# Two gated feed-forwards in fp32 on one core: the seven-product scheme in both, with adding transfers, and a row of a norm moved into the next norm's epsilon

## The chip, the cores and the metric

One core of a Trainium2 chip. The time is device microseconds of one execution, the median of the runs shown; less is better. The engines are PE (TensorE, with PEld its weight load), DVE (VectorE), ACT (ScalarE), POOL (GpSimd) and SP, which here only issues transfers.

## What is computed

Two transformer blocks one after the other on 512 tokens of width 1024 in fp32. Each ends in a gated feed-forward of inner width 2816; the rest (convolution, mLSTM, retention, attention) is not touched by the change.

```python
# first block
h = rms_norm(x, norm_ffn_g) * (1.0 + sc2) + sh2
gt, up = split(h @ w_ffn_up)
x = x + g2 * ((silu(gt) * up) @ w_ffn_down)
# second block
hn = rmsnorm(h, pre_ffn_norm)
ff = (silu(hn @ w_gate) * (hn @ w_up)) @ w_down
h = h + rmsnorm(ff, post_ffn_norm)
e = rmsnorm(p @ w_ple_proj, ple_norm)
h = h + e * sigmoid(h @ w_ple_gate + b_ple_gate)
```

`rmsnorm(x, w)` is `x * rsqrt(mean(x*x) + EPS) * w`, with EPS 1e-6.

## The kernel before

Activations lie with features on the partitions and the 512 tokens along the row. An fp32 product is made of three products of rounded halves: a weight tile of 128 x 1024 (`raw`, four buffers) is rounded by ACT into `sph`, DVE subtracts to get `spl` (L2337), and PE sums sph x high, spl x high (L1784, L1785) and sph x low (L1792) of the activations over eight k-tiles. One such **unit**, 24 matmuls of 128x512, makes one bank, that is 128 outputs of all tokens. The feed-forward's inner width is 22 tiles **f** of 128, and each f takes two units, gate and up. The results go as `midh` (MH) and `midl` (ML) into the down product.

**The seven-product scheme** runs in the first feed-forward for f = 3 to 13 (`SEVEN = {1: (3, 14)}`). It takes an f's two units as 2x2 blocks (gate and up against the two halves of k, the two halves of the tokens on the other side) and makes seven block products in place of eight: product s = 7 i + step for the i-th such f, each 12 matmuls of 128x256 (L1813, L1814, L1822). Its weight factors are half tiles: steps 0, 1 and 6 take a half as it is, steps 2 to 5 a sum of halves (`seven_sum`, DVE, L2618 to L2627, in `sums`). Each factor is then rounded (`seven_high`, ACT, L2161) and subtracted (`seven_low`, DVE, L2635). `sums` and `spl` are the same memory, a ring of six half tiles, so factor s waits for product s - 6. On the other side four sums of quarters of the activations are made once from the full activations `PF` (`seven_t_sum`, `seven_t_high`, `seven_t_low`: `ts`, `th`, `tl`). The products are joined on the way out of the banks by `seven_copy` (ACT), `seven_gate`, `seven_up` (two instructions) and `seven_last` (DVE); `seven_mid` multiplies silu(gate) by up in two halves and `seven_mid_low` (L2670) makes ML.

**What sets the order.** `plan()` writes one list of steps, and each engine runs its own in that order, waiting on semaphores. In `sevens`, at product s, `factors` adds the factor s + 5, then `drain` adds what is left of the f before, then come the joins of this f and the product itself. So DVE takes factors, joins and products of TMP in one fixed order, and anything that waits holds back all behind it. In front of the sevens, `gemms` runs f = 0 to 2 as plain units; the callback `halves(n)` of the n-th unit adds the steps that make `ts`, `th` and `tl`.

**The second feed-forward** (`ffn_up(2, ...)`) is plain throughout. It does not wait for its norm: HH and HL hold x times the gain, and the norm's row (`RROW`, one factor for each token, out of `ffn_rows`) is multiplied in afterwards, into gate before the silu (L2676) and into the product (L2689). The first three units are interleaved (`together=3`), two more follow, and then their five banks are evacuated in turn, since the row comes only then. Beside its units 4 to 12 lie `e_squares`: the eight squares (ACT) and sums (DVE, L2343) of the embedding `EE`, and a ninth call that turns the sum on PE (L1872) and takes the root.

Of the rings TMP has six rows, the main banks are five in the second feed-forward, RAW has four buffers. BY_DMA units (6 to 23, before the part that is told of here) get their `spl` by a transfer from POOL that adds into its destination (L2974).

## Time and profile before

| | us |
|---|---|
| median of 3 runs (1569.41 to 1570.70) | 1569.88 |
| the profiled execution | 1569.71 |
| its span, first to last instruction | 1567.9 |
| PE busy | 1539.4 |
| DVE busy | 1053.9 |
| ACT busy | 698.2 |
| POOL busy | 107.3 |
| sevens of the first feed-forward, 554.0 to 673.1 | 119.0 |
| same f in the second, 1186.7 to 1306.3 | 119.7 |

The profiled execution is 0.17 us under the median, and 1.8 us of it lie outside the span. A row of the timeline gives start, duration, engine, line, operation and tiles, and in brackets how long the engine had been idle and what ended that. Neighbouring instructions of one engine overlap in the records: a DVE row of 0.68 us is followed by the next after 0.60. The mean granted clock of PE was 0.997.

### The profile page before, as it was taken

Reading aid. Unit: us, or ns where it says so; the run is one execution under the profiler, and the core shown is the slowest. Engines: PE = TensorE matmul, PEld = TensorE weight load, DVE = VectorE, ACT = ScalarE, POOL = GpSimd, SP = SyncE. Lnnn points to the kernel's source line nnn. Section 1 sums busy time; section 2 is a strip of 40 time slices with the busy share of each in tenths; the row PEclk is TensorE's granted clock in tenths of the full one; section 3 lists DMA queues with packets and bytes.
Section 4 is the critical chain, followed back from the end, with each engine's and each line's share of the span. In section 5 each row is a group of like instructions: output and inputs, shape, how many; then the busy total and the mean of one; then the engine's idle time right before and its main releaser. Section 6 shows DMA issues by size and latency. Waiting matters only on the chain.

```text
span 1567.9 us, 19025 instructions
## 1 busy us (share of the span) xinstructions
PE 1539.4 (98%) x7320; PEld 1266.2 (81%) x7320; DVE 1053.9 (67%) x1631; ACT 698.2 (45%) x1025; POOL 107.3 (7%) x100
## 2 busy tenths in 40 slices
PE   8999899999999999999999999999999999999998
PEld 3788778877888899988888887778888888888877
DVE  7998898887887799954563547766486544442346
ACT  5543578764542655532233335446354332222233
POOL 0111000000000100000011001000201011000000
PEclk9999999999999999999999999999999999999999
DMA  9787222223565323344333323211333322233331
GB/s 371 177 206 183 75 88 63 83 83 118 191 242 171 131 82 96 94 142 143 102 111 101 108 84 109 66 42 41 114 112 106 105 95 94 97 95 101 98 134 67
DMA packets 54092, 185.10 MB, mean 118 GB/s; under 512 B 6381, under 2 KB 8685, under 8 KB 53746
## 3 DMA queue, kind: packets, MB, share of 16 engines
q1 hardware_dynamic: 51056, 173.39, 33.8%
q0 software_dynamic: 2944, 10.50, 3.5%
q8 instruction: 58, 0.95, 0.3%
q14 instruction: 32, 0.26, 0.0%
q10 hardware_dynamic: 2, 0.00, 0.0%
HBM read 169.70 MB, written 4.20 MB: 111 GB/s over the span
## 4 chain that ended last, share of the span: by engine, by line
PE 82%; DVE 12%; ACT 3%; issue 2%; DMA 0%; ACTq 0%; DVEq 0%; POOL 0%; POOLq 0%
PE bank L1792 23%; PE bank L1784 23%; PE bank L1785 23%; DVE convout L2391 2%; PE bank L1840 2%; DVE tmp L2462 1%; PE bank L1852 1%; PE bank L1854 1%; PE bank L1853 1%; PE bank L1927 1%; PE bank L1944 1%; DVE spl L2337 1%; DVE spl L2635 1%; PE bank L1957 1%; PE bank L1950 1%
## 5 line engine op out<-in xcount | busy, mean ns | idle before, releaser
L1784 PE MATMUL bank<-HH,sph 128*128 128x512 f32 x1256 | 499.9, 398 | 6.9 <-DVE spl L2337 4.7
L1785 PE MATMUL bank<-HH,spl 128*128 128x512 f32 x1256 | 490.7, 391 | 0.0
L2337 DVE TENSOR_TENSOR spl<-raw,sph 128x1024 fp32r<-128x1024 f32 (+1 forms) x214 | 269.4, 1260 | 238.2 <-ACT sph L2002 238.1
L1792 PE MATMUL bank<-HL,sph 128*128 128x512 f32 x1256 | 325.5, 394 | 0.0
L2002 ACT ACTIVATE sph<-raw 128x1024 fp32r<-128x1024 f32 (+1 forms) x235 | 241.5, 1029 | 177.8 <-PE bank L1792 141.2
L1784 PEld LDWEIGHTS bank<-HH,sph 128*128 128x128 f32 x1256 | 236.6, 188 | 60.7 <-issue 9.5
L1785 PEld LDWEIGHTS bank<-HH,spl 128*128 128x128 f32 x1256 | 236.7, 188 | 50.1 <-issue 1.2
L1792 PEld LDWEIGHTS bank<-HL,sph 128*128 128x128 f32 x1256 | 234.7, 188 | 51.1 <-issue 2.4
L2391 DVE SCALAR_TENSOR_TENSOR convout<-convin,vecs,convout 128x512 f32<-128x512 f32 x240 | 164.9, 742 | 0.0
L1784 PE MATMUL bank<-midh,sph 128*128 128x512 f32 x352 | 136.9, 389 | 0.0
L1785 PE MATMUL bank<-midh,spl 128*128 128x512 f32 x352 | 136.9, 389 | 0.0
L1792 PE MATMUL bank<-midl,sph 128*128 128x512 f32 x352 | 87.6, 389 | 0.0
L2204 ACT ACTIVATE midh<-tmp 128x512 fp32r<-128x512 f32 x33 | 20.9, 633 | 127.7 <-DVE tmp L2689 87.9
L1785 PEld LDWEIGHTS bank<-midh,spl 128*128 128x128 f32 x352 | 66.1, 188 | 13.7
L1792 PEld LDWEIGHTS bank<-midl,sph 128*128 128x128 f32 x352 | 66.1, 188 | 13.7
L1784 PEld LDWEIGHTS bank<-midh,sph 128*128 128x128 f32 x352 | 66.1, 188 | 13.7
L2979 POOL TENSOR_TENSOR tmp<-tmp,tmp 128x512 f32<-128x512 f32 x27 | 35.2, 1313 | 509.0 <-ACT tmp L2017 509.0
L1813 PE MATMUL bank<-th,sph 128*128 128x256 f32 x176 | 45.1, 289 | 5.6 <-DVE tmp L2652 4.3
L2462 DVE SCALAR_TENSOR_TENSOR tmp<-xpad,vecs,tmp 128x512 f32<-128x512 f32 x48 | 36.0, 749 | 16.6 <-ACT tmp L2061 15.5
L2161 ACT ACTIVATE sph<-sums 128x512 fp32r<-128x512 f32 x44 | 27.8, 632 | 38.4 <-DVE sums L2627 16.7
L3012 POOL TENSOR_TENSOR midl<-tmp,midh 128x512 fp32r<-128x512 f32 x22 | 28.5, 1296 | 230.3 <-ACT midh L2204 230.3
L1814 PE MATMUL bank<-th,spl 128*128 128x256 f32 x176 | 44.0, 283 | 0.0
(359 smaller groups left out, 2118.8 us busy)
## 6 DMA issues: line engine op xcount, KB each, us to landing
raw<-in_w_in SPq DMA_DIRECT2D x69, 512.0 KB, 3.6
raw<-in_w_up SPq DMA_DIRECT2D x66, 512.0 KB, 3.5
more<-in_w_ada SPq DMA_DIRECT2D x32, 512.0 KB, 4.7
raw<-in_w_down SPq DMA_DIRECT2D x32, 512.0 KB, 3.5
raw<-in_w_gate SPq DMA_DIRECT2D x22, 512.0 KB, 3.2
spl<-raw POOLq DMA_DIRECT2D x18, 512.0 KB, 6.0
ada<-in_w_ada SPq DMA_DIRECT2D x16, 512.0 KB, 11.3
raw<-in_w_down SPq DMA_DIRECT2D x16, 384.0 KB, 3.1
```

Source lines behind the costliest of these rows:

```text
L1784: e.matmul(P_[b][:], sph(n)[:, q], hi[:, k, :], start=k == 0, stop=False)
L1785: e.matmul(P_[b][:], spl(n)[:, q], hi[:, k, :], start=False, stop=False)
L1792: m = e.matmul(P_[b][:], sph(n)[:, q], low[:, k, :], start=False, stop=last and k == kb - 1)
L1813: e.matmul(to, high_of(which, s)[:, q], x, start=k == 0, stop=False)
L1814: e.matmul(to, low_of(which, s)[:, q], x, start=False, stop=False)
L1840: m = e.matmul(P_[b][:], raw(n)[:, token(k)], FULL[acts][:, k, :], start=k == 0, stop=k == 7)
L2002: e.activation(sph(n), raw(n), ACT.Copy).then_inc(*up("s_w_high", ("wh", n)))
L2337: e.tensor_tensor(spl(n), raw(n), sph(n).bitcast(F32), ALU.subtract).then_inc(*up("s_w_low", ("wl", n)))
L2391: ins = e.scalar_tensor_tensor(CO[:, i, :], src, wt, CO[:, i, :], ALU.mult, ALU.add)
L2462: e.scalar_tensor_tensor(TMP[j][:], XP[:, s, k:k + 512], wt, TMP[j][:], ALU.mult, ALU.add).then_inc(*up("s_qk_conv", ("qk_conv", h, z, k)))
L2979: e.tensor_tensor(TMP[a][:], TMP[a][:], TMP[j][:], ALU.add).then_inc(*up("s_sum_p", ("ss", name, i)))
L3012: e.tensor_tensor(ML[:, i, :], TMP[j][:], MH[:, i, :].bitcast(F32), ALU.subtract).then_inc(*up("s_cut_p", ("lo", "m2", i)))
```

## The change

1. `SEVEN` gets the second feed-forward too, for the same f = 3 to 13. `PF` is there x times the gain (ACT, 8 instructions), DVE makes `ts` and `tl`, ACT `th`, as in the first. In `seven_gate` and `seven_last` the norm's row is multiplied in on half the width each (`seven_scaled`).
2. Of the four weight sums three remain. The sum of the two first halves is made by a transfer that POOL issues, which adds one half onto the other in `raw` (`seven_third`, 256 KB for each f). The signs of some factors are turned, and `seven_mid` multiplies by -1 in the same instruction. The second factor's low part now waits for the third sum, because both use the memory of the first sum.
3. `seven_mid_low` leaves DVE: ACT writes -MH into ML and a transfer from POOL adds TMP to it (256 KB for each f).
4. In the second feed-forward the row is no longer multiplied into the up side. So the down product is off by a factor for each token, which its own norm takes out again once its epsilon is EPS times (mean(x*x) + EPS) of the norm before: `ff_eps` keeps that in `KEEP`, and the root of `ff` adds it in place of EPS.
5. `e_squares` moves from units 4 to 12 into the sevens: steps 1, 3 and 5 of the first three f. `EE` moves by 4096 bytes.

```diff
-SEVEN = {1: (3, 14)}
-SEVEN_SUMS = (2, 3, 4, 5)
-SEVEN_BANK = ((0, 0), (1, 0), (2, 1), (1, 1), (3, 1), (2, 0), (3, 0))
+SEVEN = {1: (3, 14), 2: (3, 14)}
+SEVEN_SUMS = (2, 3, 4)
+SEVEN_BANK = ((0, 0), (1, 0), (1, 1), (2, 1), (3, 1), (2, 0), (3, 0))
...
             add("seven_high", st["which"], s)
-            if s:
+            if s % 7 == 4:
+                factor_low(st, s - 2)
+            if s and s % 7 != 3:
                 factor_low(st, s - 1)
...
+            if step == 5 and i + 2 < f1 - f0:
+                add("seven_third", which, i + 2)
+            if which == 2 and i < 3 and step in (1, 3, 5):
+                e_squares()
...
         def halves(n):
-            if n == 1:
+            if n in (3, 5):
+                add("seven_third", which, (n - 3) // 2)
+            if which == 2 and n < 2:
+                for i in range(4 * n, 4 * n + 4):
+                    add("seven_full", which, i)
+            elif n == 1:
                 for i in range(0, 8, 2):
                     add("seven_full", which, i)
+            if n == 1:
                 add("seven_t_sum", which, 0)
...
             def seven_low(which, s):
                 w.wait_ge(at("seven_high", which, s))
+                if s % 7 == 2:
+                    w.wait_ge(at("seven_sum", which, s + 2))
...
+                if which == 2:
+                    w.wait_ge(at("seven_gate", 2, i), at("rrow", 2))
+                    e.tensor_tensor(TMP[j][:, 0:256], TMP[j][:, 0:256], RROW[:, 0:256], ALU.mult).then_inc(
+                        *up("s_ffn", ("seven_scaled", i, 0)))
...
-                    e.tensor_tensor(TMP[j][:], TMP[j][:], P_[b][:], ALU.mult).then_inc(*up("s_ffn", ("up", 2, i)))
-                    w.wait_ge(at("up", 2, i))
-                    e.tensor_tensor(TMP[j][:], TMP[j][:], RROW[:], ALU.mult).then_inc(
-                        *up("s_ffn", ("up_done", 2, i)))
+                    e.tensor_tensor(TMP[j][:], TMP[j][:], P_[b][:], ALU.mult).then_inc(
+                        *up("s_ffn", ("up", 2, i), ("up_done", 2, i)))
...
+            def seven_third(which, i):
+                n = seven_at[which][0] + 2 * i
+                w.wait_ge(at("raw", n), at("raw", n + 1))
+                e.dma_start(raw_half(n + 1, 0), raw_half(n, 0), accum_op=ALU.add).then_inc(
+                    *G.up(f"d_third{i % 2}", ("seven_third", which, i), by=16))
+
+            def seven_mid_low(which, i, f, j):
+                w.wait_ge(at("less", f"m{which}", f))
+                e.dma_start(ML[:, f, :], TMP[j][:], accum_op=ALU.add).then_inc(
+                    *G.up(f"d_mid{f % 4}", ("lo", f"m{which}", f), by=16))
```

Where instructions now stand, in three places. `raw` and `spl` carry the number of their buffer.

DVE at the start of the second feed-forward, before: from the product of f = 0 on, its evacuations and the first of the sums of `EE`.

```order
L2687 TENSOR_TENSOR tmp_91<-tmp_91,bank 128x512 [waits s_gate,s_product]
L2689 TENSOR_TENSOR tmp_91<-tmp_91,rrow 128x512 [waits s_ffn]
L2676 TENSOR_TENSOR tmp_90<-bank,rrow 128x512 [waits s_product]
L2687 TENSOR_TENSOR tmp_90<-tmp_90,bank 128x512 [waits s_gate,s_product]
L2689 TENSOR_TENSOR tmp_90<-tmp_90,rrow 128x512 [waits s_ffn]
L2676 TENSOR_TENSOR tmp_88<-bank,rrow 128x512 [waits s_product]
L2337 TENSOR_TENSOR spl_63<-raw_56,sph_60 128x1024 [waits s_w_high]
```

The same engine and place in the changed kernel, from the product of f = 0 to the low part of factor 1 (the last row).

```order
L2726 TENSOR_TENSOR tmp_91<-tmp_91,bank 128x512 [waits s_gate,s_product]
L2633 TENSOR_TENSOR ts<-pf 128x1024 [waits s_cut_a,s_w_low]
L2715 TENSOR_TENSOR tmp_90<-bank,rrow 128x512 [waits s_product]
L2636 SCALAR_TENSOR_TENSOR ts<-pf,ts 128x1024 [waits s_cut]
L2726 TENSOR_TENSOR tmp_90<-tmp_90,bank 128x512 [waits s_gate,s_product]
L2646 TENSOR_TENSOR tl<-ts,th 128x1024 [waits s_cut_a]
L2641 SCALAR_TENSOR_TENSOR ts<-pf,ts 128x1024 [waits s_cut]
L2715 TENSOR_TENSOR tmp_88<-bank,rrow 128x512 [waits s_product]
L2646 TENSOR_TENSOR tl<-ts,th 128x1024 [waits s_cut_a]
L2638 TENSOR_TENSOR ts<-pf 128x1024
L2655 TENSOR_TENSOR sums_66<-raw_56 128x512 [waits d_third0,d_raw2]
L2671 TENSOR_TENSOR spl_62<-raw_55,sph_59 128x512 [waits s_w_high]
```

Six instructions of 1024 columns and two waits on other engines (`s_cut_a` is ACT, `d_third0` the transfer) now stand between the evacuation of f = 0 and the low part of factor 1. Behind the last row follow the sum for factor 3, one product, two more `tl`, the third sum, and only then the low part of factor 2.

ACT at the same place, before: the silu of each gate and the high part of each product.

```order
L2199 ACTIVATE tmp_91<-tmp_91 128x512 [waits s_ffn]
L2204 ACTIVATE midh<-tmp_91 128x512 [waits s_w_low,s_w_high,s_ffn]
L2199 ACTIVATE tmp_90<-tmp_90 128x512 [waits s_ffn]
L2204 ACTIVATE midh<-tmp_90 128x512 [waits s_ffn]
L2199 ACTIVATE tmp_88<-tmp_88 128x512 [waits s_ffn]
```

And in the changed kernel.

```order
L2223 ACTIVATE tmp_91<-tmp_91 128x512 [waits s_ffn]
L2156 ACTIVATE pf<-XT,vecs 128x512 [waits s_w_low,s_w_high]
L2156 ACTIVATE pf<-XT,vecs 128x512 x3
L2228 ACTIVATE midh<-tmp_91 128x512 [waits s_ffn]
L2156 ACTIVATE pf<-XT,vecs 128x512 x4
L2223 ACTIVATE tmp_90<-tmp_90 128x512 [waits s_ffn]
L2165 ACTIVATE th<-ts 128x1024 [waits s_cut]
```

The eight `pf` stand behind the first silu and in front of the second, and the first `ts` on DVE waits for all of them.

DVE in the second feed-forward beside the sums of `EE` (L2343), before: each sum stands between the split of a whole unit and an evacuation.

```order
L2337 TENSOR_TENSOR spl_61<-raw_57,sph_58 128x1024 [waits s_w_high]
L2676 TENSOR_TENSOR tmp_86<-bank,rrow 128x512 [waits s_product]
L2343 TENSOR_TENSOR tmp_87<-tmp_87,tmp_89 128x512 [waits s_sum,s_square]
L2337 TENSOR_TENSOR spl_62<-raw_54,sph_59 128x1024 [waits s_w_high]
L2687 TENSOR_TENSOR tmp_86<-tmp_86,bank 128x512 [waits s_gate,s_product]
L2689 TENSOR_TENSOR tmp_86<-tmp_86,rrow 128x512 [waits s_ffn]
```

In the changed kernel they (now L2367) stand between the factors of the sevens; here most of the second f of the sevens.

```order
L2367 TENSOR_TENSOR tmp_87<-tmp_87,tmp_90 128x512 [waits s_sum,s_square]
L2655 TENSOR_TENSOR sums_64<-raw_56 128x512 [waits d_third0,d_raw2,s_product]
L2671 TENSOR_TENSOR spl_63<-raw_55,sph_60 128x512 [waits s_w_high]
L2676 TENSOR_TENSOR tmp_88<-tmp_86,bank 128x512 [waits s_gate]
L2682 TENSOR_TENSOR tmp_88<-tmp_88,rrow 128x256 [waits s_ffn]
L2658 TENSOR_TENSOR sums_64<-sums_64,raw_55 128x512 [waits s_w_low,d_raw1,s_product]
L2367 TENSOR_TENSOR tmp_87<-tmp_87,tmp_89 128x512 [waits s_sum,s_square]
L2661 TENSOR_TENSOR sums_65<-raw_55,sums_64 128x512 [waits s_product]
L2671 TENSOR_TENSOR spl_61<-sums_64,sph_58 128x512 [waits s_w_low,s_w_high]
L2671 TENSOR_TENSOR spl_61<-sums_64,sph_58 128x512 [waits s_w_high]
L2687 TENSOR_TENSOR tmp_86<-tmp_88,bank 128x512
```

Each waits for a square on ACT, and all factors of the f behind it wait with it. On PE the turn of the finished sum, which waits for the last of them, stands in front of product 19, step 5 of the third f.

## Rows read from the trace of the kernel before

**Rows 1.** The page, first part: busy time and share of the span.

```profile
PE 1539.4 (98%) x7320; PEld 1266.2 (81%) x7320; DVE 1053.9 (67%) x1631; ACT 698.2 (45%) x1025; POOL 107.3 (7%) x100
```

**Rows 2.** Windows: from:to, length, then busy time of each engine, clock, transfers.

```profile
554.00:673.00 119.00, 113.35 (x925) 111.31 (x924) 111.77 (x192) 62.89 (x117) 0.00 (x0) 1.00 0.32 98
1187.00:1306.00 119.00, 119.00 (x529) 98.52 (x528) 60.64 (x67) 42.77 (x57) 15.12 (x12) 1.00 0.29 98
```

**Rows 3.** The chain of waits in order: start, length; ends of two neighbouring units.

```profile
1184.84 1.81 PE bank L1792 x8
1190.28 1.81 PE bank L1792 x8
```

**Rows 4.** Timeline of PE in the sevens: products 0, 1 and 3, first unit behind.

```profile
554.02 0.28 PE L1813 MATMUL bank<-HH,sph 128*128 128x256 f32 x1
...
555.45 0.28 PE L1813 MATMUL bank<-HH,sph 128*128 128x256 f32 x1
...
559.82 0.39 PE L1813 MATMUL bank<-th,sph 128*128 128x256 f32 x1 [1.34 <-DVE spl L2635]
...
673.05 0.40 PE L1784 MATMUL bank<-HH,sph 128*128 128x512 f32 x1
```

**Rows 5.** Waits of PE in the sevens: us in total, times, longest.

```profile
PE bank L1813 <- DVE tmp L2652: 4.3, 9, 0.5
```

**Rows 6.** Timeline of DVE, one round of the sevens.

```profile
614.42 0.69 DVE L2635 TENSOR_TENSOR spl<-raw,sph 128x512 fp32r<-128x512 f32 x1 [0.41 <-ACT sph L2161]
615.03 0.42 DVE L2662 TENSOR_TENSOR tmp<-tmp,tmp 128x256 f32<-128x256 f32 x1
615.37 0.42 DVE L2665 TENSOR_TENSOR tmp<-tmp,tmp 128x256 f32<-128x256 f32 x1
```

**Rows 7.** Timeline of DVE at the start of the sevens: sum and low part.

```profile
558.48 0.69 DVE L2624 TENSOR_TENSOR sums<-raw,sums 128x512 f32<-128x512 f32 x1
559.09 0.68 DVE L2635 TENSOR_TENSOR spl<-sums,sph 128x512 fp32r<-128x512 f32 x1
```

**Rows 8.** Timeline of the first gate of the second feed-forward, DVE and ACT.

```profile
1180.17 0.69 DVE L2676 TENSOR_TENSOR tmp<-bank,rrow 128x512 f32<-128x512 f32 x1
1180.90 0.63 ACT L2199 ACTIVATE tmp<-tmp 128x512 f32<-128x512 f32 x1 [2.19 <-DVE tmp L2676]
```

**Rows 9.** Timeline of the first feed-forward, the instructions that make PF, TS and TH.

```profile
536.28 2.55 ACT L2143 ACTIVATE pf<-pf,mod 128x512 f32<-128x512 f32 x4
...
539.11 1.22 DVE L2596 TENSOR_TENSOR ts<-pf 128x1024 f32<-128x1024 f32 x1 [2.01 <-ACT pf L2143]
540.25 1.22 DVE L2337 TENSOR_TENSOR spl<-raw,sph 128x1024 fp32r<-128x1024 f32 x1
...
540.37 1.06 ACT L2148 ACTIVATE th<-ts 128x1024 fp32r<-128x1024 f32 x1
```

**Rows 10.** The page: POOL's ML; transfers (KB, median us to landing).

```profile
L3012 POOL TENSOR_TENSOR midl<-tmp,midh 128x512 fp32r<-128x512 f32 x22 | 28.5, 1296 | 230.3 <-ACT midh L2204 230.3
...
raw<-in_w_up SPq DMA_DIRECT2D x66, 512.0 KB, 3.5
...
spl<-raw POOLq DMA_DIRECT2D x18, 512.0 KB, 6.0
...
tmp<-m_scratch POOLq DMA_DIRECT2D x4, 256.0 KB, 4.1
```

**Rows 11.** Sums of EE in 1187 to 1306 by form; and the reciprocal behind them.

```profile
L2343 DVE TENSOR_TENSOR tmp<-tmp,tmp 128x512 f32<-128x512 f32 x7 | 7.5, 1078 | 8.5 <-ACT tmp L2017 8.5
...
1227.69 0.18 DVE L2359 RECIPROCAL small<-small 128x4 f32<-128x4 f32 x1 [1.42 <-ACT small L2022]
```

**Rows 12.** The longest wait of PE within the kernel, and the windows behind it.

```profile
179.03 0.76 PE L1784 MATMUL bank<-HH,sph 128*128 128x512 f32 x1 [4.74 <-DVE spl L2337]
...
180.00:182.00 2.00, 2.00 (x6) 1.59 (x5) 1.83 (x7) 0.00 (x0) 0.00 (x0) 0.50 0.70 248
184.00:186.00 2.00, 2.00 (x10) 1.66 (x9) 1.90 (x5) 1.97 (x4) 0.47 (x1) 1.00 0.00 0
```

More of the change, by code:

```diff
@@ L165, in split @@
     def split():
-        n = W["cut"]
+        c = n = W["cut"]
         for st in stages:
-            if st["first"] <= n < st["first"] + st["slots"]:
-                factors(st, 2 * (n - st["first"]) + 2)
+            if st["first"] <= c < st["first"] + st["slots"]:
+                factors(st, 2 * (c - st["first"]) + 2)
                 W["cut"] += 1
                 return
-            if n >= st["first"] + st["slots"]:
+            if c >= st["first"] + st["slots"]:
                 n -= st["slots"] - st["units"]
@@ L426, in rsqrt @@
         add("rsqrt", name, src, v, q, r, n, scale, after)
+        if name == "x4":
+            add("ff_eps", v)
         return r
@@ L945, in ffn_up @@
             jobs += part(i)
-        if which == 2:
-            jobs = [(*job[:3], e_squares) if 4 <= n < 13 else job for n, job in enumerate(jobs)]
         if not st:
@@ L977, in ffn_up @@
             gemm(src, tile_no, 8, acts, evac)
-            if n % 2:
+            if n % 2 and which == 1:
                 ada_more(1 if ada_at[0] < 32 else 0)
@@ L1520, in program @@
         PTL = place("ptl", B + 8192, [128, 2, S], F32R)
-        EE = place("ee", B + 16384, [128, 8, S])
+        EE = place("ee", B + 12288, [128, 8, S])
         PTS_0 = place("pts0", B + 65536, [128, 2, S])
@@ L2141, in seven_full @@
             def seven_full(which, i):
+                if which == 2:
+                    w.wait_ge(at("x", 4, i), *fenced("f2"))
+                    e.activation(PF[:, i, :], XT[:, i, :], ACT.Copy, scale=vec("g_pf", i)).then_inc(
+                        *up("s_cut_a", ("full2", i)))
+                    return
                 w.wait_ge(at("lo", "n2", i))
@@ L2158, in seven_high @@
                 else:
-                    w.wait_ge(at("raw", n if s % 7 < 2 else n + 1))
+                    w.wait_ge(at("seven_third", which, s // 7) if s % 7 == 5 else at("raw", n if s % 7 < 2 else n + 1))
                     given = undivided(which, s)
@@ L2180, in seven_mid @@
                 w.wait_ge(at("seven_mid", which, i), *fenced(f"f{which}"))
+                if which == 2:
+                    w.wait_ge(at("e_spilt"))
                 e.activation(MH[:, f, :], TMP[j][:], ACT.Copy).then_inc(*up("s_cut_a", ("hi", f"m{which}", f)))
+            def seven_mid_low(which, i, f, j):
+                w.wait_ge(at("hi", f"m{which}", f))
+                e.activation(ML[:, f, :], MH[:, f, :].bitcast(F32), ACT.Copy, scale=-1.0).then_inc(
+                    *up("s_cut_a", ("less", f"m{which}", f)))
             def gmix(i):
@@ L2616, in seven_sum @@
                 if s % 7 == 2:
-                    w.wait_ge(at("raw", n + 1))
+                    w.wait_ge(at("raw", n + 1), at("seven_third", which, s // 7))
                     ins = e.tensor_tensor(to, raw_half(n + 1, 0), raw_half(n + 1, 1), ALU.add)
```

73 lines of the change are left out of this document (42 added, 31 removed).

## The prediction

> **What bounds the kernel now.** I read the busy shares first. PE is busy 98% of the span [rows 1], so a gain must come out of PE's work or of one of its few gaps. Next I compared two windows of equal length with the same eleven tiles f = 3 to 13: the first feed-forward with the seven-product scheme, the second without it [rows 2]. The reader is to see two different limits. In the second PE has no gap (119.0 of 119.0), and DVE is half idle (60.6). In the first PE lacks 5.7 us, and DVE is busy 111.8 of 119.0: the scheme takes matmuls from PE and gives DVE almost all that it can do. The timeline of PE [rows 4] and its waits [rows 5] say who holds it: ten gaps, all ended by DVE.
>
> **Prices of PE.** A plain unit takes 5.44 us (1184.84 to 1190.28, [rows 3]), an f two of them, 10.88. A product of the scheme takes 1.44 us (554.02 to 555.45, [rows 4]), an f seven, 10.08. Eleven f: 119.7 against 110.9. So the scheme is worth 8.8 us in a feed-forward, if nobody waits.
>
> **First feed-forward.** It took 119.0 us (554.02 to 673.05, [rows 4]), so 8.1 over 110.9. Of these 1.5 came before product 3, which began at 559.82 and not at 558.34; the other 6.6 are DVE's. From product 3 on, 74 products took 113.2 us, 10.7 for each f: that is DVE's round. An instruction of 512 columns takes 0.60 us of it from start to start (558.48 to 559.09, [rows 7]), one of 256 columns 0.34 [rows 6]. The change takes out one weight sum and the ML instruction, 1.2 us, so the round falls to some 9.5, under PE's 10.08, and the 6.6 us go. In exchange the low part of factor 2 must wait for the third sum. That sum stood at 558.48 [rows 7], behind the last `tl`, and I find nothing that moves it; the low part then ends at about 559.8, and product 2 begins there and not at 556.9. Product 3 follows at 561.25, 1.4 later than before. Gain 5.2 us. Bounds: 3 (a round nearer 10.08, or a cold clock after the wait of 2.9 us, below) to 6.6.
> The two new transfers for each f lie beside this. ACT has room for its extra instruction (62.9 of 119, [rows 2]). For the landing of 256 KB the trace has two neighbours, 4.1 us for a plain transfer of that size and 6.0 for an adding one of twice the size [rows 10]; I take 4.5 and keep 4.1 to 6.0. The last factor of an f frees the second raw buffer, its load lands 3.5 us later [rows 10], and by the plan the sum that needs the added half comes some 8 us behind that: hidden.
> The Trainium skill (DMA: Bandwidth & Descriptors, "Anatomy of one DMA — SWDGE (gpsimd) path") fits such a transfer as 2.0 us plus its bytes over 436 GB/s, an estimate of 2.6 us here. The row of 6.0 us for 512 KB is nearly twice what that fit gives (3.2), so the trace disagrees; by the page the sum would be 0.8 us lower, in the next part.
>
> **Second feed-forward, start.** It gains 8.8 us by PE's prices. But the order shows what stands in front of its first products. The first gate is scaled by the norm's row at 1180.2, and its silu ends at 1181.5 [rows 8]. Only then does ACT take the eight `pf` (0.64 each, from 2.55 for four, [rows 9]) and one high part: 5.6 us, to 1187.1. The first `ts` waits for all eight. From there DVE has eleven instructions to the low part of factor 1: six of 1024 columns at 1.14 (539.11 to 540.25, [rows 9]) and five at 0.60, 9.8 us, to 1197.0. The added half comes somewhat later still: POOL issues it behind its second ML (1.3 us, [rows 10]), which waits for the high part of f = 1 at about 1191.4, so at 1192.8, and lands it at 1197.3; with 0.8 us for that, factor 1 is ready at 1197.8. PE finishes the last plain unit at 1186.65 [rows 3], product 0 at 1188.1, and waits 9.7 us.
> Then come one sum, one product of TMP and one `tl` (2.4 us), a wait of 0.6 for the last `th`, which ACT makes (1.06, [rows 9]) behind two factors and a high part, the last `tl`, the third sum and the low part of factor 2 (2.3): 1203.1. Product 2 was due at 1189.5. **Loss 13.6 us**; bounds 12.4 (`pf` at 0.53, the added half in time) to 15.5 (it lands after 6.0).
>
> **The sums of EE.** From product 2 of the first f to product 2 of the fourth DVE decides, so I add up its rounds, low part of factor 2 to low part of factor 2. Without EE a round has 13 instructions at 0.60, five halves at 0.34 (two are the new scaling), some 0.4 for steps that depend on the one before, and the wait of 0.4 for ACT [rows 6]: 10.3. Each sum of EE adds 0.60 and a wait for its square, which stands on ACT behind factors. Before, that wait was 1.2 on average (8.5 over 7, [rows 11]) and cost nothing. The first round has no joins of an f before it and stays inside PE's 10.08, with 0.7 to spare. Following the rows of the second, with three sums, I find waits of 0.9, 1.6 and 1.2 for their squares, in place of the 0.4: 15.4. In the third a root with its trip to ACT (1.4, [rows 11]) stands for one sum: 16.0. Together 31.4 against 20.2, less 0.7: **loss 10.5 us**, 5 of it at one place, where PE is to turn the finished sum in front of product 19 and waits for the last sum. Bounds 6 (no wait for squares) to 15 (their waits half as long again). Behind the third f the round of 10.3 costs up to 0.2 for each of eight f, less what the cold clock gives DVE: 0.5, bounds 0 to 3.
>
> **The clock.** After PE's wait of 4.74 us the granted clock was 0.50, 1.2 of 2.4 GHz, and 1.00 again at 184 [rows 12]; a window of 2 us held 6 matmuls in place of 10, so some 4.4 us at half pace, about 2.2 us lost. In the changed kernel two waits are as long or longer, 9.7 us and 5. I take 3.5 for both, since part of the first is hidden by the wait before product 2; bounds 0 to 6.6 with the first feed-forward's.
>
> **Epsilon.** In the plain f one DVE instruction goes and one tiny one is added; DVE is half idle there [rows 2], so nothing. What it spares in the sevens is counted above.
>
> **Sum**, against the profiled execution's 1569.7, which is the median within 0.2: -5.2 - 8.8 + 13.6 + 10.5 + 0.5 + 3.5 = +14.1, **1583.8 us**.
>
> **Rivals.** A: the scheme pays in both, because DVE and ACT find time that I don't see: -5.2 - 8.8 gives 1555.7. For it speaks that DVE is half idle in the second window; against it that the start is a fixed order with the row at 1180.2, and no idle time of the average can be moved in front of that.
> B: only the start costs, and the sums of EE slip into waits that PE has anyway: -14.0 + 13.6 + 1 gives 1570.3. Against it: after product 2 PE and DVE run at the same pace, so an instruction more on DVE is a wait on PE.
> C (slower than the forecast): the added halves come late in every f. By the 8 us above, it decides at a landing of about 8 us; at 9.5 us, 1.5 us in each of 20 f, 30 us, 1613. Against it: beside a DVE that was almost never idle, 512 KB landed in 6.0 [rows 10].
> The Trainium skill (GPSIMD Engine Reference, the table of its specifications) says that GpSimd shares its SBUF interfaces with VectorE and contends with instructions that have two SBUF inputs, which most here are. By that rule C gains; the trace shows no such delay in the rows of 6.0.
>
> **How the numbers follow.** Forecast 0.72, A 0.08, B 0.14, C 0.06. The forecast's own bounds: the gains 14.0 against 12.4 + 6 gives 1574.1, 11.8 against 15.5 + 15 + 3 + 3.5 gives 1595, with all bad ends together. The range must reach B and may leave out A, C and the last of the bad ends: 1570 to 1592. A measurement of this kernel can tell about 0.2%, 3.1 us, from no change. Faster than 1566.7: A and a little of B, 0.10. Within: most of B, 0.13. Slower than 1573.0: 0.77.
>
> **What would show it.** Right: in the first sevens no more gaps ended by the second half of `seven_up` (L2652 before), one gap of 2.9 us before product 2 and an end near 113.8 us after the start; in the second a gap of 9 to 10 us before product 1 ended by DVE, one of 3 to 4 before product 2, one of about 5 at the turn of EE's sum, a clock of 0.50 behind the first, and 135 to 142 us for the eleven f. Wrong: product 1 soon after 1188, gaps ended by a DMA in every f, or a DVE round in the first sevens that stays at 10.7.

## The result, and the profile after

| | before | changed |
|---|---|---|
| median of 4 runs each | 1569.64 us | 1593.41 us |
| lowest to highest | 1568.89 to 1570.70 | 1592.59 to 1593.88 |
| ratio | | 1.0148, 95% interval 1.0135 to 1.0160 |

The changed kernel is slower by 23.8 us. The forecast was +14.1 (1583.8), its range ended at 1592.0: direction and places were right, the sum was 9.6 us short.

The page of the changed kernel, first part (compare [rows 1]): PE has hardly more work, DVE and ACT have 47 us more each.

```profile
PE 1540.1 (97%) x7716; PEld 1285.2 (81%) x7716; DVE 1101.4 (69%) x1750; ACT 744.9 (47%) x1136; POOL 131.2 (8%) x133
```

Its windows over the two sevens (columns as in [rows 2]; the last three numbers are granted clock, share of the transfers, GB/s): the first are filled by PE, in the second PE lacks 23 us, DVE is busy in 125 of 145, and the mean clock is 0.92.

```profile
555.00:671.00 116.00, 113.03 (x928) 112.75 (x927) 101.81 (x172) 67.71 (x129) 16.33 (x19) 0.99 0.57 144
1184.00:1329.00 145.00, 121.58 (x931) 118.42 (x929) 124.57 (x212) 79.73 (x148) 20.70 (x23) 0.92 0.46 117
```

PE's waits from 1184 to 1332 (us in total, times, longest). Every one was ended by DVE, none by a transfer, and L2652's nine in the first sevens [rows 5] are gone.

```profile
PE bank L1825 <- DVE spl L2671: 15.9, 3, 10.2
PE bank L1884 <- DVE tmp L2367: 5.0, 1, 5.0
PE bank L1825 <- DVE tmp L2676: 2.0, 1, 2.0
PE bank L1796 <- DVE spl L2361: 1.5, 1, 1.5
```

The timeline of PE puts them in place. The rows are product 0 and 2 of the first sevens and the unit behind these (compare [rows 4]); then of the second sevens product 0, 1, 2, 9, 15, 16, the turn of EE's sum ahead of product 19, product 23, and the first plain unit behind.

```profile
555.39 0.28 PE L1825 MATMUL bank<-HH,sph 128*128 128x256 f32 x1
...
561.39 0.39 PE L1825 MATMUL bank<-th,sph 128*128 128x256 f32 x1 [2.97 <-DVE spl L2671]
...
670.98 0.40 PE L1796 MATMUL bank<-HH,sph 128*128 128x512 f32 x1
...
1184.43 0.28 PE L1825 MATMUL bank<-HH,sph 128*128 128x256 f32 x1
...
1196.22 0.55 PE L1825 MATMUL bank<-HH,sph 128*128 128x256 f32 x1 [10.20 <-DVE spl L2671]
...
1202.08 0.58 PE L1825 MATMUL bank<-th,sph 128*128 128x256 f32 x1 [2.96 <-DVE spl L2671]
...
1214.72 0.28 PE L1825 MATMUL bank<-th,sph 128*128 128x256 f32 x1
...
1225.55 0.38 PE L1825 MATMUL bank<-HH,sph 128*128 128x256 f32 x1 [2.03 <-DVE tmp L2676]
...
1229.97 0.39 PE L1825 MATMUL bank<-th,sph 128*128 128x256 f32 x1 [2.74 <-DVE spl L2671]
...
1239.73 0.69 PE L1884 MATMUL bank<-consts,tmp 128*128 128x128 f32 x2 [4.97 <-DVE tmp L2367]
...
1248.43 0.28 PE L1825 MATMUL bank<-th,sph 128*128 128x256 f32 x1
...
1330.42 0.50 PE L1796 MATMUL bank<-HH,sph 128*128 128x512 f32 x1 [1.54 <-DVE spl L2361]
```

**Where the 23.9 us between the two profiles lie.** I cut every profile at the same four marks of PE: product 0 of the first sevens; the first matmul of the first down product; the turn of the second norm's sums (the four small matmuls ahead of the second feed-forward); the first matmul of the second down product. A is the stretch between the first two, B between the last two.

| us | product 0 at | A | between | B | behind |
|---|---|---|---|---|---|
| before | 554.02 | 206.10 | 414.53 | 219.05 | 174.20 |
| changed | 555.39 | 202.66 | 414.52 | 245.02 | 174.21 |

So -3.4 in A, +26.0 in B, and +1.4 ahead of product 0. That last piece isn't the change's: in kernels that are the same up to there product 0 stood between 553.2 and 555.4.

**B by rows of PE.** 77 products at 1.44 would be 110.9, 8.8 under before. From product 0 to product 2 it took 17.65, 14.8 more than two products; from 2 to 23 46.35, 16.1 more than 21; from 23 to the end of 76 (1328.71) 80.28, 2.5 more; and 1.5 of gap behind. -8.8 + 14.8 + 16.1 + 2.5 + 1.5 = +26.1.

### The profile page after: what moved, and what is told of

Read it like the earlier page. It is cut to its first block, busy times and chain, and to the rows that moved or that the text cites. A ratio compares the mean times of both kernels' runs of the same rounds, so it can differ in the third digit from the quotient of the medians.

```text
span 1591.8 us, 20216 instructions
## 1 busy us (share of the span) xinstructions
PE 1540.1 (97%) x7716; PEld 1285.2 (81%) x7716; DVE 1101.4 (69%) x1750; ACT 744.9 (47%) x1136; POOL 131.2 (8%) x133
## 4 chain that ended last, share of the span: by engine, by line
PE 79%; DVE 13%; ACT 4%; issue 2%; DMA 1%; ACTq 0%; DVEq 0%; POOL 0%; POOLq 0%
PE bank L1796 20%; PE bank L1804 20%; PE bank L1797 20%; PE bank L1825 2%; PE bank L1834 2%; PE bank L1826 2%; DVE convout L2425 2%; PE bank L1852 2%; DVE spl L2671 2%; DVE tmp L2496 1%; PE bank L1864 1%; PE bank L1866 1%; PE bank L1865 1%; PE bank L1939 1%; DVE spl L2361 1%
## 5 line engine op out<-in xcount | busy, mean ns | idle before, releaser
L1796 PE MATMUL bank<-HH,sph 128*128 128x512 f32 x1080 | 431.3, 399 | 8.8 <-DVE spl L2361 6.4
L1797 PE MATMUL bank<-HH,spl 128*128 128x512 f32 x1080 | 422.0, 391 | 0.0
L1804 PE MATMUL bank<-HL,sph 128*128 128x512 f32 x1080 | 282.0, 395 | 0.0
L1825 PE MATMUL bank<-th,sph 128*128 128x256 f32 x352 | 93.0, 295 | 9.1 <-DVE spl L2671 8.7
L1826 PE MATMUL bank<-th,spl 128*128 128x256 f32 x352 | 91.5, 290 | 0.0
L1825 PEld LDWEIGHTS bank<-th,sph 128*128 128x128 f32 x352 | 70.1, 199 | 11.6 <-DVE spl L2671 10.6
L1825 PE MATMUL bank<-HH,sph 128*128 128x256 f32 x264 | 67.3, 287 | 12.2 <-DVE spl L2671 10.2
L1826 PEld LDWEIGHTS bank<-th,spl 128*128 128x128 f32 x352 | 70.2, 200 | 0.0
L1826 PE MATMUL bank<-HH,spl 128*128 128x256 f32 x264 | 66.9, 285 | 0.0
L2671 DVE TENSOR_TENSOR spl<-raw,sph 128x512 fp32r<-128x512 f32 x88 | 60.2, 688 | 7.8 <-ACT sph L2178 7.5
```

Of the source, the lines that this page charges most:

```text
L1796: e.matmul(P_[b][:], sph(n)[:, q], hi[:, k, :], start=k == 0, stop=False)
L1797: e.matmul(P_[b][:], spl(n)[:, q], hi[:, k, :], start=False, stop=False)
L1804: m = e.matmul(P_[b][:], sph(n)[:, q], low[:, k, :], start=False, stop=last and k == kb - 1)
L1825: e.matmul(to, high_of(which, s)[:, q], x, start=k == 0, stop=False)
L1826: e.matmul(to, low_of(which, s)[:, q], x, start=False, stop=False)
L2671: e.tensor_tensor(low_of(which, s), given, high_of(which, s).bitcast(F32), ALU.subtract).then_inc(*up("s_w_low", ("seven_low", which, s), ...
```

## The experiments

All are compared with the kernel before, on the same chip. For sevens that begin one f later A begins 10.88 later too; in the table that is added.

| kernel | median us | ratio to before, 95% | A | B |
|---|---|---|---|---|
| e1_first_only | 1566.45 | 0.9975 (0.9966 to 0.9985) | 201.17 | 219.08 |
| e2_no_sums | 1578.31 | 1.0051 (1.0036 to 1.0066) | 201.16 | 231.48 |
| e3_warm | 1592.27 | 1.0141 (1.0126 to 1.0156) | 201.17 | 247.02 |
| e4_early | 1590.35 | 1.0127 (1.0112 to 1.0142) | 202.65 | 243.04 |
| e5_warm_turn | 1589.97 | 1.0131 (1.0116 to 1.0146) | 201.16 | 243.48 |
| e6_no_scale | 1584.27 | 1.0098 (1.0083 to 1.0113) | 202.67 | 237.57 |
| e7_late_second | 1574.51 | 1.0026 (1.0013 to 1.0039) | 203.70 | 226.22 |
| e8_late_first | 1563.39 | 0.9959 (0.9945 to 0.9974) | 199.69 | 219.07 |
| e9_sums_later | 1586.69 | 1.0104 (1.0089 to 1.0119) | 202.65 | 238.95 |
| e10_both_late | 1570.29 | 1.0002 (0.9993 to 1.0011) | 199.68 | 225.75 |
| e11_row_on_pool | 1574.71 | 1.0033 (1.0020 to 1.0046) | 199.69 | 229.58 |
| e12_from_five | 1577.72 | 1.0048 (1.0031 to 1.0064) | 199.68 | 234.03 |
| e13_silu_later | 1588.90 | 1.0115 (1.0098 to 1.0132) | 202.44 | 240.02 |
| e14_from_five | 1564.67 | 0.9965 (0.9952 to 0.9978) | 199.70 | 220.23 |
| e15_from_eight | 1562.83 | 0.9951 (0.9936 to 0.9966) | 199.70 | 216.98 |
| e16_turn_later | 1559.66 | 0.9932 (0.9920 to 0.9944) | 199.69 | 214.56 |
| e17_five_turn_later | 1565.93 | 0.9972 (0.9961 to 0.9983) | 199.69 | 221.63 |

### Which half of the change costs: e1

```diff
-SEVEN = {1: (3, 14), 2: (3, 14)}
+SEVEN = {1: (3, 14)}
...
+        if which == 2:
+            jobs = [(*job[:3], e_squares) if 4 <= n < 13 else job for n, job in enumerate(jobs)]
```

> The second feed-forward plain again, with the sums of EE back in its units 4 to 12; all the rest of the change stays (adding transfers in the first feed-forward, the row moved into the epsilon). Theory: everything lost was lost in the second sevens. The first sevens take 115.6 us as in the changed kernel (119.0 before), the second feed-forward is as before, and the 1.4 us by which the first sevens start later in the profile of the change stay if they come from the change: 1567.5, or 1566.2 if they don't. Rival: the transfers or the epsilon cost something outside the sevens: 1570 or more.

Measured 1566.45, B as before: the whole loss is the second sevens', and transfers and epsilon cost nothing outside them. A is 4.9 under before, not 3.4. PE waits the same 2.97 before product 2 as in the changed kernel, but here the clock did not fall:

```profile
563.00:565.00 2.00, 2.00 (x19) 2.00 (x18) 1.78 (x4) 0.43 (x1) 0.00 (x0) 1.00 0.36 74
```

The changed kernel in the same window: 0.50, 11 matmuls for 19.

```profile
563.00:565.00 2.00, 2.00 (x11) 2.00 (x11) 1.35 (x3) 0.72 (x2) 0.00 (x0) 0.50 0.34 94
```

So the difference of 1.5 us is the clock alone. The time lies at the 1566.2 of the expectation: the later start of product 0 is not the change's.

### The sums of EE: e2 and e9

e2 drops the calls of `e_squares`. e9 keeps them; in `e_sum` the sum of square i - 1 (`sum_held`) now goes with square i:

```diff
-        for i in range(8):
-            sse.add(("EE", i), [("e", i)])
...
+        for i in range(1, 8):
+            sum_held()
+            j, free = tmp.take()
+            add("square", "e", i, j, free, ("EE", i), [("e", i)], None)
+            held.append((i, j))
             yield
+        sum_held()
```

> The changed kernel with the squares and sums of EE left out (and its root; the last norm is spread from a kept column that does not belong to it, so the output of that norm isn't the reference's). Theory: the rounds of the second and third f lose 5.2 and 8.4 us to these sums, 2.2 of it by the cold clock behind the third wait; without them 1593.4 - 13.6 = 1579.8. Rival: DVE is too slow in the second sevens even without them, since the rounds of the later f are 10.65 us where PE needs 10.08; then the first rounds stay long and the time is above 1585.

> The changed kernel; at each of its nine places in the second sevens the square of EE is followed by the sum of the square before it, not by its own. Nothing is left out. Theory: in the trace of the change DVE stands idle 0.9 to 1.7 us in front of seven of these sums, for a square that ACT makes just ahead of it (8.9 us together), and that is more than half of what EE costs there; only the sums' own 0.6 us and the root stay: rounds of about 12 and 14.5 us for 16.0 and 16.7, time 1586, bounds 1584 to 1588. Rival: DVE's own instructions are what the rounds lack; the waits only move in front of other rows (TMP, high parts): 1590 or more.

Both came out close to their theories (1578.31 for 1579.8, 1586.69 for 1586). e2 took 13.5 us from B: EE is the largest part of what the rows between product 2 and 23 lose (46.35 became 32.43, and 21 products without a wait are 30.2). The late rounds stayed as slow as they were, so its rival is right about those alone. e9 took 6.1 from B. In the timeline of DVE in the changed kernel one sees what it removed: an idle time in front of each sum, for a square that ACT has only just begun (7 such, 8.9 us; before, 8.5 over 7 that cost nothing, [rows 11]).

```profile
1206.23 0.69 DVE L2367 TENSOR_TENSOR tmp<-tmp,tmp 128x512 f32<-128x512 f32 x1 [1.19 <-ACT tmp L2029]
...
1223.00 0.69 DVE L2367 TENSOR_TENSOR tmp<-tmp,tmp 128x512 f32<-128x512 f32 x1 [1.66 <-ACT tmp L2029]
...
1238.98 0.69 DVE L2367 TENSOR_TENSOR tmp<-tmp,tmp 128x512 f32<-128x512 f32 x1 [1.65 <-ACT tmp L2029]
```

In e9 PE runs from product 2 to 18 without a gap, where the changed kernel has two (in front of 15 and 16). The only wait of PE that EE still causes is the turn in front of product 19, now 5.7 us, with a cold clock behind it (waits of PE, 1180 to 1330):

```profile
PE bank L1840 <- DVE spl L2686: 13.7, 3, 10.2
PE bank L1899 <- DVE tmp L2382: 5.7, 1, 5.7
PE bank L1811 <- DVE spl L2376: 1.6, 1, 1.6
```

### The clock: e3 and e5

`warm_seven` is a row of matmuls into a bank that is free there; in e5 the 20 for product 19 stand ahead of `e_squares()`:

```diff
+            if (which, s) in WARM:
+                add("warm_seven", wb, wfree, WARM[which, s])
```

> The changed kernel with matmuls that nobody reads, of 512 columns at 0.23 us, put on PE ahead of the products that wait: 11 before product 2 of the first sevens, and in the second 42 before product 1, 18 before product 2, 8, 11 and 20 before products 15, 16 and 19. Theory: the cold clock behind the waits costs 1.6 + 4.0 + 2.2 = 7.8 us; a clock that stays at 1.00 gives these back, less what DVE then holds up since it loses the time in which it got ahead: 1586 to 1589. Rival (the forecast's own size): the clock costs 3.5, the rest is DVE's anyway: 1590 or more.

> As e3_warm, but the 20 matmuls stand ahead of the turn of EE's sum, where PE waits 5.0 us, and not behind it. In e3_warm they stood behind it and took 4.5 us themselves, and the wait stayed cold. Theory: the cold clock costs 1.5 in the first sevens, 1.6 net at the start of the second (of 4.0 in the rows of PE the rounds with EE give 2.4 back, since DVE holds them anyway) and 2.2 behind the turn: 1593.4 - 5.3 = 1588.1, 4 us under e3_warm. Rival: behind the turn too the time belongs to DVE; then only the wasted matmuls of e3_warm show in neither place and the time stays at 1590.3.

Both kept the clock at 1.00 behind the waits for products 1, 2, 15 and 16, as e5's window behind the first wait shows (the changed kernel's: 0.50 with 8 matmuls). At the turn only e5 did: in e3 PE waited 4.96 us there, the clock fell to 0.50 (1234 to 1238), and the 20 matmuls behind the turn ran cold themselves.

```profile
1196.00:1198.00 2.00, 2.00 (x10) 1.67 (x9) 1.93 (x2) 0.00 (x0) 1.06 (x2) 1.00 0.22 40
```

Behind each of its rows of unread matmuls e5's PE still waited 0.1 to 0.7 us for DVE, so they held nothing up. Yet B fell by only 1.5 in e5, and in e3 it rose by 2.0. The rows of PE show why. Products 3 and 4 take 1.44 again in e5, but the rounds behind are as long as before or longer: from product 2 to 23 42.96 against 46.35, and from 23 on 82.1 against 80.3, since PE now reaches sooner the pace that DVE can hold. Both theories missed (1592.27 for at most 1589, 1589.97 for 1588.1), and both rivals came true: I had taken the cold products from PE's rows and added them to waits which they partly replace. The cold clock costs 3.0 us in the whole kernel (1.5 in A, 1.5 in B), not 5.3 and not 7.8.

### DVE's round: e6, e13 and e11

e6 leaves the two multiplications by the row out. e13 leaves nothing out and moves one silu on ACT:

```diff
             if step == 0:
                 add("seven_last", which, i, banks[3][0], up[i])
+                if which == 1:
+                    add("seven_silu_last", which, i, up[i])
+            elif step == 1:
+                if which == 2:
+                    add("seven_silu_last", which, i, up[i])
```

> The changed kernel without the two multiplications by the norm's row in each f of the second sevens (their silu takes the unscaled gate, so the output isn't the reference's). Theory: a round of DVE there is 10.65 us against PE's 10.08, and the two scalings are 0.7 of it; without them the round is below PE's, and the 2.5 us that the last 33 products lose go: 1590.9. Rival: the round is held by the wait for ACT's high part (0.40) and a chain that does not shorten: 1592.5 or more.

> The changed kernel with ACT's silu of the second half of the gate one product later in the second sevens, so that it stands behind the high part that DVE waits for. Nothing is left out. Theory: DVE's round of 10.65 us holds 0.40 of waiting for that high part, because ACT waits for the scaled gate first; without it the round is 10.25, the 2.5 us that the last 33 products lose fall under 1, and the gap of 1.5 in front of the first plain unit, which comes from the same lateness, shrinks: 1593.4 - 3 = 1590.4, bounds 1589 to 1591.5. Rival: the product of TMP two steps on then waits for the later silu, and the round stays: 1593.

e6 took 7.5 from B and e13 5.0, more than either theory gave. In both PE has no gap from product 21 on, and from product 23 to 76 runs at 1.44 each; the gap behind the sevens is gone in e6 and 1.1 in e13. Another 3.1 us of e6 and 2.0 of e13 came from the rounds with EE (rows of PE from product 2 to 23), which are DVE's too. What e13 removed is this wait in DVE's round of the changed kernel (the row with the bracket; [rows 6] has the same wait, 0.41, in the kernel before). The other two rows are the scalings.

```profile
1302.74 0.42 DVE L2701 TENSOR_TENSOR tmp<-tmp,rrow 128x256 f32<-128x256 f32 x1
...
1304.17 0.69 DVE L2671 TENSOR_TENSOR spl<-raw,sph 128x512 fp32r<-128x512 f32 x1 [0.40 <-ACT sph L2178]
...
1308.07 0.42 DVE L2682 TENSOR_TENSOR tmp<-tmp,rrow 128x256 f32<-128x256 f32 x1
```

e13 has the same two low parts back to back:

```profile
1298.83 1.28 DVE L2676 TENSOR_TENSOR spl<-raw,sph 128x512 fp32r<-128x512 f32 x2
```

In the changed kernel ACT stands 2.9 us in front of that silu, waiting for the scaled gate, and the high part comes behind it. So DVE waits for ACT, which waits for DVE.

e11 takes the same two instructions off DVE by giving them to POOL:

> e10_both_late with the two multiplications by the norm's row in each f of the second sevens on POOL instead of DVE. Theory (after e6_no_scale, which gave 9.1 us without them): DVE's round falls below PE's 10.08, so neither the late rounds nor the gap behind the sevens cost anything: 3 us under e10_both_late, 1557. Rival: POOL's instruction is slower and holds its two transfers and the silu behind it, or slows DVE beside it: no gain on e10_both_late, or a loss of 1 us in each f.

The theory (1557) missed by 17.7 us. It was 4.4 us slower than e10 and B 3.8 longer, the rival's case. Two lines of the groups by form, 1220 to 1305, show one part of it: the sum that runs beside POOL's instruction. Of e10:

```profile
L2691 DVE TENSOR_TENSOR sums<-raw,sums 128x512 f32<-128x512 f32 x8 | 5.5, 684 | 0.0
```

and of e11, where it took 1162 ns:

```profile
L3042 POOL TENSOR_TENSOR tmp<-tmp,rrow 128x256 f32<-128x256 f32 x7 | 7.7, 1100 | 4.4 <-DVE tmp L2706 4.4
...
L2691 DVE TENSOR_TENSOR sums<-raw,sums 128x512 f32<-128x512 f32 x8 | 9.3, 1162 | 0.0
```

The other part is the chain: POOL's 1.1 us stands for DVE's 0.42 ahead of the silu, and DVE then waits 1.6 for the high part behind it. The Trainium skill (GPSIMD Engine Reference, the table of its specifications) says that GpSimd's SBUF interfaces are shared with VectorE and that instructions with two SBUF inputs contend; the trace agrees, 1162 ns for 684. It also shows that not every such pair is slow (timeline of e11, rows of DVE and POOL):

```profile
1250.44 0.68 DVE L2688 TENSOR_TENSOR sums<-sums,raw 128x512 f32<-128x512 f32 x1
1250.62 1.10 POOL L3042 TENSOR_TENSOR tmp<-tmp,rrow 128x256 f32<-128x256 f32 x1
1251.04 1.23 DVE L2691 TENSOR_TENSOR sums<-raw,sums 128x512 f32<-128x512 f32 x1
...
1255.84 0.69 DVE L2701 TENSOR_TENSOR spl<-raw,sph 128x512 fp32r<-128x512 f32 x1
1256.01 1.11 POOL L3048 TENSOR_TENSOR tmp<-tmp,rrow 128x256 f32<-128x256 f32 x1 [3.47 <-DVE tmp L2723]
```

The two DVE instructions that had begun ahead of POOL's took their usual time; the one that began 0.68 us before the end of POOL's took 0.54 longer.

### The starts: e4, e8, e7, e10, e12

e4, in `ffn_rows`:

```diff
         r = root_of(ss, D)
+        for i in range(8):
+            add("seven_full", 2, i)
+        add("seven_t_sum", 2, 0)
+        add("seven_t_sum", 2, 1)
```

e8, on top of e1 (10 f don't fill the ring of three weight slots evenly, so one slot is passed over):

```diff
-SEVEN = {1: (3, 14)}
+SEVEN = {1: (4, 14)}
```

> The changed kernel with the eight copies PF of the second feed-forward issued behind the squares of its norm, ahead of the first gate, the first two sums TS behind them, and TH, TL, the other TS and the first two adding transfers one unit earlier. Theory: the start of the second sevens costs 13.2 us of waits and 4.0 of clock because PF stands behind the first silu; 11 us earlier, one short wait is left and most of it goes: 1593.4 - 13 = 1580, bounds 1577 to 1584. Rival: the adding transfer, behind POOL's ML, is what ends last once DVE is early: a wait of 5 us or more stays before product 1, and the time is 1586 or more.

> e1_first_only with the sevens of the first feed-forward over f = 4 to 13 instead of 3 to 13; TS, TH and TL stay at their units, so they stand two units further ahead. Theory: the wait of 3.0 us before product 2 and the 1.6 of cold clock behind it are the work of the start not done in time; both go, one f less costs 0.8: 1566.4 - 3.8 = 1562.6. Rival: product 2 waits for the order of the new scheme itself (its low part behind the third sum), however early the start: 1566.4 + 0.8 = 1567.2.

e8 came close to its theory (1563.39 for 1562.6, -3.1 against e1 for -3.8). Its one wait of 0.7 before product 2 stands for 2.97. e4 missed (1590.35 for 1580): B fell by 2.0 and not by 13. The first TS stood on DVE waiting 5.0 for PF, ahead of the copy of the norm's row and with it of the first gate; the banks came free late, and PE stood in a plain unit instead (timeline of PE in e4):

```profile
1184.07 0.80 PE L1807 MATMUL bank<-HH,sph 128*128 128x512 f32 x1 [5.05 <-DVE tmp L2726]
```

and 5.3 more before product 1, since DVE had 12 us of work from there to the low part of factor 1. The time is in the rival's range, but not for its reason: DVE did not wait for the added half. So the start's price was not that PF came late: it was a mass of DVE work between the row and product 1. That called for more plain units ahead:

> The whole change, but the second sevens run over f = 6 to 13 only; EE's squares and sums stand in plain units 3 to 11, PF at units 1 and 2, TS, TH and TL at units 3 to 7. Theory: with twelve plain units ahead DVE has done the start's work beside them; no long wait of PE is left in the second feed-forward, and eight f give 6.4 us, of which up to 2.5 go to the DVE round of 10.65 and 1.5 to the gap in front of the first plain unit behind. Against the first feed-forward alone (1566.4): 1564, bounds 1561 to 1566. Rival: the start's waits come from the scheme itself (the adding transfer, the last TL) and not from the units ahead: 1569 or more.

> The whole change with the first sevens over f = 4 to 13 and the second over f = 6 to 13, EE's squares at plain units 2 to 10 and each sum one unit behind its square. Theory: in e7_late_second DVE stood idle 1.2 us in front of every sum of EE and 1.9 in front of TS, and its split stood behind that: PE waited 2.8 and 0.9 in plain units and 2.2 before product 2, since EE's root stood there too. All these go; what stays is the DVE round of 10.65 in the last f and the gap of 1.5 behind the sevens. Against e8_late_first: 1563.4 - 6.4 + 3 = 1560, bounds 1558 to 1563. Rival: TS, TL and the splits overfill DVE in the plain units whatever the order: 1565 or more.

> e11_row_on_pool with the second sevens from f = 5 on and EE's squares, TS, TH and TL one unit earlier. Theory: one f more in the scheme is worth 0.8 us as long as DVE finds the time ahead of it: 1556.2. Rival: the ten plain units are too few, a wait with its cold clock comes back in them or before product 2: 1559 or more.

All three missed, by 10.5, 10.3 and 21.5 us. The gap moved once more, to the plain units; e7's timeline of PE:

```profile
1192.09 0.47 PE L1811 MATMUL bank<-HH,sph 128*128 128x512 f32 x1 [2.84 <-DVE spl L2376]
```

There DVE waited for PF in front of TS, with the split of the next unit behind; in e10 the split itself waited for a high part that stood on ACT behind PF and TH (PE 3.4 late), and in e12, where DVE stood 6.8 us for PF, PE's wait in the plain unit was 6.4. On top came 2.2 before product 2 and 2.5 behind the sevens in e7, 1.4 at EE's turn and 2.5 behind the sevens in e10, and 1.6, 2.3 and e11's 0.85 in most f in e12.

### Can the second sevens pay: e14 to e17

These put four of the eight PF ahead of the norm's root, where ACT stands idle for 4 us, spread the rest over two units, and keep e9's order of the sums and e13's silu. e16 and e17 also turn EE's sum a unit later, in `e_sum`:

```diff
         sum_held()
+        yield
         b = sse.columns()
```

> The whole change with the first sevens over f = 4 to 13, the second over f = 5 to 13, and the silu as in e13. Of PF four are made ahead of the norm's root, where ACT stands idle for 4 us, the rest at units 0 and 1; EE's squares at units 1 to 9, each sum a unit later, TS, TH and TL at units 2 to 6. Theory: in e10 DVE waited 2.4 us for PF and then for a high part behind it, and PE 3.4 for that; and the sevens' padded length made the first unit behind wait for the last product (2.5). With both gone nine f give 7.2 us less 1 to 2 of drift: against e8's 1563.4, 1557.5, bounds 1556 to 1561. Rival: ten plain units hold too little of DVE's time for the start, EE and the splits: a wait of 3 us or more in them, 1563 or more.

> As e14_from_five, with the second sevens over f = 8 to 13: sixteen plain units ahead of them, EE's squares at units 4 to 12, TS, TH and TL at units 3 to 7, and no padding. Theory: nothing waits, six f give 4.8 us and DVE's longer round doesn't come through in so few: 1558.6, bounds 1557.5 to 1560.5. Rival: the plain units with TS, TL and a sum of EE are overfull (2 splits' worth more on DVE than 5.44 us hold), whatever stands behind them: 1562 or more.

> e15_from_eight with EE's squares two units earlier, the turn of its finished sum one unit behind the last sum and not right behind it, and TS, TH and TL one unit later. Theory: the gain of the six f, 4.8 us, came to only 2.1 in e15 since PE waited 1.4 for the last sum of EE in front of its turn and 0.4 for a split behind the first TS, with a cold clock behind; both go: 217.0 us from the turn of the norm's sums to the down product become 214.5, the time 1560.5. Rival: a plain unit with TS, TL and EE in it holds more DVE work than PE needs for it, and the same time is lost at another unit: 1562.5 or more.

> The same for the second sevens from f = 5 on (nine f): EE's squares from unit 0, the turn at unit 9, TS, TH and TL at units 3 to 7. Theory: e14 lost 2.9 at the turn, 1.9 in a plain unit and 1.5 to 2 by cold clocks; with these gone nine f give 7.2 us: 1558, bounds 1557 to 1561. Rival: in ten plain units EE, TS, TL and the splits together are too much for DVE: 1563 or more.

e16 met its theory (1559.66 for 1560.5); e14, e15 and e17 missed by 7.2, 4.2 and 7.9 us, and their rivals came true. e16 is the best kernel of all: 10.4 us under before, 33.8 under the change as made, and in its second feed-forward, from 1170 to 1380, PE waits for nobody. Its B, 214.56, is 4.5 under before, where six f by PE's prices are worth 4.8; another 6.4 are A's, which e8 has too without any sevens in the second feed-forward (1563.39). e14 and e17 show the other side: three f more are worth 2.4, but with ten plain units ahead, in place of sixteen, the waits come back (1.9 and 2.9 in e14; 1.6 and 3.3 in e17).

## Why the prediction was wrong, point by point

**First feed-forward (-5.2).** Right. Without the clock's fall A is 4.9 shorter, the wait before product 2 was 2.97 for the 2.9 forecast, and DVE no longer sets the pace. With the fall it is 3.4.

**Second feed-forward, PE's prices (-8.8).** Right: 1.44 for each product wherever nobody waits.

**Landing of the added half (4.5).** Under-sized, without effect. The two new transfers' medians in the changed kernel:

```profile
raw<-raw POOLq DMA_DIRECT2D x22, 256.0 KB, 5.3
midl<-tmp POOLq DMA_DIRECT2D x22, 256.0 KB, 3.2
```

5.3 lies inside the bounds of 4.1 to 6.0, and no wait of PE was ended by it; the longest took 7.6, so rival C's limit of 8 us was not reached. The estimate by the Trainium skill (DMA: Bandwidth & Descriptors, "Anatomy of one DMA — SWDGE (gpsimd) path"), 2.6 us, is half of it.

**Start (+13.6).** Right in place and nearly in size: waits of 10.20 and 2.96 where 9.7 and 3.4 were worked out, together 13.2. With the cold product between them product 2 came 14.8 late. That is DVE's time and not the clock's: e5 held the clock and took the same 17.7 us to product 2. Two errors met here, so part of the agreement is luck. DVE did not wait for the added half, for which the forecast had 0.8. And beside POOL's ML DVE's third TS took 2.29 where the second took 1.22, 1.1 that the forecast did not have.

```profile
1186.85 1.22 DVE L2636 SCALAR_TENSOR_TENSOR ts<-pf,ts 128x1024 f32<-128x1024 f32 x1
...
1189.40 1.52 POOL L3059 TENSOR_TENSOR midl<-tmp,midh 128x512 fp32r<-128x512 f32 x1 [5.61 <-ACT midh L2228]
1189.72 2.29 DVE L2641 SCALAR_TENSOR_TENSOR ts<-pf,ts 128x1024 f32<-128x1024 f32 x1
```

**The sums of EE (+10.5) and the drift (+0.5): the step that failed.** The mechanism was right, waits for the squares of 0.93, 1.66 and 1.28 in the second round (forecast 0.9, 1.6 and 1.2) and the turn of 5 (4.97), but the base under it was mis-sized. The forecast took DVE's round as 10.3. It is 10.65 (each f from product 51 on in the changed kernel, and every late f in e5), and PE's is 10.08 (the same f in e6 and e13). A late round of DVE, low part to low part (1304.17 to 1314.82), shows which terms were too small:

```profile
1306.05 0.68 DVE L2655 TENSOR_TENSOR sums<-raw 128x512 f32<-128x512 f32 x1
1306.75 0.69 DVE L2671 TENSOR_TENSOR spl<-raw,sph 128x512 fp32r<-128x512 f32 x1
...
1309.02 0.68 DVE L2661 TENSOR_TENSOR sums<-raw,sums 128x512 f32<-128x512 f32 x1
1309.81 1.29 DVE L2671 TENSOR_TENSOR spl<-sums,sph 128x512 fp32r<-128x512 f32 x2
...
1313.73 0.69 DVE L2671 TENSOR_TENSOR spl<-raw,sph 128x512 fp32r<-128x512 f32 x1
1314.82 0.69 DVE L2671 TENSOR_TENSOR spl<-raw,sph 128x512 fp32r<-128x512 f32 x1 [0.40 <-ACT sph L2178]
```

The count of instructions was right. But five steps depend on one just before, and start 0.70 to 0.79 behind it where 0.60 was taken: together 0.6 and not "some 0.4". And the wait for ACT costs 0.49 (1313.73 to 1314.82, less 0.60): its bracket of 0.40 counts from the end of a record of 0.69, the price of 0.60 from start to start. The waits for the squares lose 0.09 each in the same way.

That 0.35 returns in every round in which DVE sets the pace. With the clock held (e5) the rows read 12.7 between product 2 and 23 for the forecast's 10.5, 4.3 for 0.5 behind, and 1.5 for a gap in front of the first plain unit that the forecast did not have: 7.5 us too much. Behind product 23 the 0.35 makes 2.7 of the 3.8 too much, and the rest is what the forecast let a cold clock give back. Between 2 and 23 e5's three rounds took 10.28, 15.99 and 16.68 where 9.4 (10.08 less "0.7 to spare"), 15.4 and 16.0 were added up. The first had no 0.7 to spare: two sums stand in it with 2.5 us of waits for squares (1.19, 1.28). The gap of 1.5 comes of the same lateness: it is gone in e6 and 1.1 in e13.

**The clock (+3.5).** All of it was put in the second feed-forward; there it cost 1.5 by e5, and 1.5 more in the first, where the forecast had it only as a bound. The cold products in the rows sum to 7.7, but more than half of that stands where DVE would have held PE.

**Epsilon (0).** Right (e1: B 219.08 for 219.05). But it left the row to be multiplied in on DVE inside the sevens, and these two half-wide instructions for each f, with the wait on ACT that they bring, cost 7.5 us of B by e6 (9.1 between the medians).

**The sum.** Forecast against measured: first feed-forward -5.2 against -3.4; second +19.3 against +26.0 (7.5 for DVE's round and what follows from it, 1.2 for the start, less 2.0 for the clock); ahead of both 0 against +1.4. Together 9.9 us. The forecast's own bad ends gave 1595; the range stopped at 1592, and the time fell between the two. What stays open is why the stretch ahead of product 0 varies by 2 us, in kernels that don't differ there.

## What to carry to other kernels

Where two engines run within a few per cent of one pace, add up the round of the slower one from a timeline that has its waits and dependent steps in it, since each 0.1 us returns in every round and in every wait behind. A lump of work that must be done before a new stage can't be hidden by moving it as a lump: count how much of the busy engine each unit ahead can hold, put single pieces there, and let no in-order engine stand in front of a piece that isn't ready (square now, its sum a unit later). Price a cold clock by holding it warm, not by the rows of the cold instructions.
